# Differential and latent attention encoder on one core: score pairs, statistics without a diagonal, rotary halves summed in the contraction

## The chip, the cores and the metric

The kernel runs on one core of a Trainium2 chip. The metric is the time on the device in microseconds (us) from one launch to its end. PE is the matrix engine (PEld its weight loads), DVE the vector engine, ACT the scalar engine, POOL is GpSimd, SP the queue that issues the transfers.

## The reference

Two layers over 512 positions of width 1024, all in float32. Cut to what matters here:

```python
u = _rmsnorm(h, g_mix[l]); z = u @ w_in[l]
# latent group, 8 heads: 64 plain + 32 rotary columns per head
q = concat([q[..., :64], _rope(q[..., 64:], cos, sin)])
k = concat([kv[..., :64], broadcast(k_rope)])          # one rotary key for all heads
o_mla = softmax(q @ k.T * 96**-0.5) @ v
# differential group, 4 heads, two maps of 64 columns each
s = dq @ dk.T * 64**-0.5 - slope * abs(qpos - kpos)    # for map 0 and map 1
w = softmax(s[0]) - lam * softmax(s[1])
o = _rmsnorm(w @ dv, g_sub[l], 1e-5) * (1 - lam_init)
h = h + concat([o_mla, o_diff]) @ w_out[l]
h = h + square(relu(_rmsnorm(h, g_mlp[l]) @ w_up[l])) @ w_down[l]
```

`_rope(x)` is `[x1*cos - x2*sin, x1*sin + x2*cos]`. `lam` is one number per layer. A final norm follows the second layer.

## The kernel before

Every float32 product is made of three products of halves: an operand is split into a high part and the rest (`_hi`, `_lo`), and `three` (line 1145) issues hi*hi, hi*lo and lo*hi. Channels lie on the partitions and the 512 positions on the columns, so most matmuls are 128x128 stationary by 512 columns. The weights come block by block through two staging buffers; ACT writes the high half (line 520), DVE the low one (line 767).

A layer has these parts in time: projections of the latent compressions and of the values; the attention, as 48 steps of one head and one tile of 128 queries (steps 0 to 15 are the differential heads, 16 to 47 the latent ones); the rest of the output projection; the MLP. The order on each engine is written out by hand. In attention step n of the differential part, the engines do:

- PE, in program order: the scores of map 0 of step n+2 (`scores_diff(l, n + 2, 0)`), in some steps the broadcast of a statistic (`stat_b`), the filler work of the step (`FILL[n]`: projections of later heads, 12 matmuls in steps 0 to 7, 6 or none in later ones), in some steps the values of a head (`values`), the four transposes of step n-1 (`turn`, line 1206), the scores of map 1 of step n+2, in some steps the column sums of a statistic (`stat_c`, line 1159). In the latent part the scores of step n+2 (`scores`) stand first. Each map's scores are three matmuls with 64 rows: map 0 in partitions 0 to 63, map 1 in 64 to 127.
- DVE: `coef` (reciprocals of the two row sums, and lambda applied to the second, lines 810 and 811), two `ttr` (bias, negation and row extreme, line 803; each frees a score bank through `sc_free`), `weights` (line 817, after POOL), the low half of a transposed map (`lo_pt`, line 837), and the reading out of filler results (`gen`, `gen_low`).
- ACT: the high half of a transposed map (`hi_pt`, line 550), two exponentials (line 531), and its part of the fillers.
- POOL: `t1` (line 481) scales the second map by its coefficient; `power` (line 475) makes the inverse root of a statistic.

Three score banks and two transpose banks are shared by all steps. Two more banks take the fillers in turn, so that a filler waits (`taken`) until the result before it in its bank is read out.

A statistic is made in this chain: `stat_c` on PE, `stat_col` on DVE, `power` on POOL, `stat_diag` on DVE (line 788: four multiplications of the identity by a column, into `diag`), `stat_b` on PE (line 1168: ones times `diag`, 128x512), and the row is read out. It occurs 8 times in a layer; four of them are the norms of the differential heads, whose `stat_c` is at the end of steps 7, 11, 15 and 19 and whose `stat_b` is in steps 9, 13, 17 and 21.

For each latent head the query is read out by three DVE operations (`gen` with use "q"): a product of 96 rows with a table, a product of the 32 swapped rotary rows with the table (line 863), and the sum of the two (line 866).

`link` makes an instruction of DVE wait for the end of the one before it.

Of the kernel before, what the change touches and what calls it, by code (L numbers as in the profile page):

```python
# [12 lines left out]
P = 128  # L13
# [163 lines left out]
CHAIN = 3 + DSTEPS  # L177

def trunk(nc, x, w_in, g_mix, g_q, g_kv, w_uq, w_ukv, lam_q1, lam_k1, lam_q2, lam_k2,
# [53 lines left out]
    diag = place("diag", [P, TT, P], F32)  # L233
# [18 lines left out]
    with ExitStack() as ctx:  # L252
# [26 lines left out]
        pow_done, diag_ready = counter("pow_done", 4 + DIFF_HEADS), counter("diag_ready", 4 + DIFF_HEADS)  # L279

        c_ready, c_hi_made, c_lo_made = (counter(n, 2 * KC) for n in ("c_ready", "c_hi_made", "c_lo_made"))
        kr_half, kr_ready = counter("kr_half", 1), counter("kr_ready", 1)
# [5 lines left out]
        qf_ready, q_hi_made, q_lo_made = (counter(n, MLA_HEADS) for n in ("qf_ready", "q_hi_made", "q_lo_made"))  # L288
# [72 lines left out]
        def q_tile(hd):  # L361

            return q_pack[0:QK, (hd + 1) % 2, 0, :], q_pack[0:QK, (hd + 1) % 2, 1, :]
# [96 lines left out]
        def _(pool):  # L460
# [30 lines left out]
            for l in layers(pool):  # L491
                power(l, MISC_AT["mix_c"], 0, rs_mix)
                power(l, MISC_AT["q_c"], 1, rs)
                power(l, MISC_AT["kv_c"], 2, rs)
                for n in range(1, STEPS + 1):
                    if n <= DSTEPS:
                        t1(l, n - 1)
                    else:
                        normalise(l, n - 1 - DSTEPS)
                    g, r = divmod(n - 8, TT)  # L500
                    if r == 0 and 0 <= g < DIFF_HEADS:
                        power(l, MISC_AT[f"sub{g}_c"], 3 + g, rs)
                power(l, MISC_AT["mlp_c"], 3 + DIFF_HEADS, rs)
# [4 lines left out]
        def _(act):  # L508
# [44 lines left out]
            def gen(l, use):  # L553
# [75 lines left out]
            for l in layers(act):  # L629
# [32 lines left out]
                for n in range(STEPS + 5):  # L662
# [14 lines left out]
                    if n in (DSTEPS - 4, DSTEPS + 3):  # L677
                        for p in (0, 1) if n == DSTEPS - 4 else (2, 3):

                            act.wait_ge(kr_ready, val(kr_ready, l, 1))  # L680
# [3 lines left out]
                            nc.scalar.activation(k_pack[NOPE:QK, p, 0, :], krf[NOPE:QK, :], ACT.Copy  # L684
                                                 ).then_inc(krb_hi_made, 1)
                            if p:
                                act.wait_ge(krb_lo_made, val(krb_lo_made, l, 1))
                                nc.scalar.activation(k_pack[NOPE:QK, p, 1, :], k_pack[NOPE:QK, 0, 1, :].bitcast(F32),
                                                     ACT.Copy).then_inc(krb_copied, 1)
# [58 lines left out]
        def _(dve):  # L748
# [91 lines left out]
            def gen(l, use):  # L840
# [17 lines left out]
                elif use[0] == "q":  # L858
# [3 lines left out]
                    nc.vector.tensor_tensor(tmp_y[0:QK, 0, :], b[0:QK, :], tabq[0:QK, :], ALU.mult)  # L862
                    nc.vector.tensor_tensor(tmp_y[NOPE:QK, 1, :], b[QK:P, :], tabq[QK:P, :], ALU.mult
                                            ).then_inc(freed(use), 1)
                    dve.wait_ge(*read_out(l, use))
                    nc.vector.tensor_tensor(tmp_y[NOPE:QK, 0, :], tmp_y[NOPE:QK, 0, :], tmp_y[NOPE:QK, 1, :], ALU.add
                                            ).then_inc(qf_ready, 1)

            def gen_low(l, use):
# [21 lines left out]
                elif use[0] == "q":  # L891
                    hd = int(use[1:])
                    dve.wait_ge(q_hi_made, val(q_hi_made, l, hd + 1))
                    nc.vector.tensor_tensor(q_tile(hd)[1], tmp_y[0:QK, 0, :], q_tile(hd)[0].bitcast(F32), ALU.subtract
# [47 lines left out]
            for l in layers(dve):  # L942
# [6 lines left out]
                stat_diag(l, 0, rs_mix)  # L949
                stat_row(l, MISC_AT["mix_b"], rb[:, :])  # L950
                for k, use in enumerate(LATENT_USES):
# [7 lines left out]
                    else:  # L959
                        if l == 0:  # L960
# [13 lines left out]
                                                ).then_inc(kr_ready, 1)  # L974
                    split(l, k + RING)
                for b in range(TT):
                    split(l, BLOCK_AT[("dv", b)] + RING)
                    if b == 0:
# [4 lines left out]
                        stat_diag(l, 1, rs)  # L983
# [6 lines left out]
                    if b == 2:  # L990
# [5 lines left out]
                        stat_diag(l, 2, rs)  # L996
# [27 lines left out]
                for n in range(STEPS + 5):  # L1024
# [32 lines left out]
                    if n == DSTEPS - 4:  # L1057
                        dve.wait_ge(krb_hi_made, val(krb_hi_made, l, 1))
                        nc.vector.tensor_tensor(k_pack[NOPE:QK, 0, 1, :], krf[NOPE:QK, :],
                                                k_pack[NOPE:QK, 0, 0, :].bitcast(F32), ALU.subtract  # L1060
# [7 lines left out]
                    if r == 0 and 0 <= g < DIFF_HEADS:  # L1068
                        stat_diag(l, 3 + g, rs)
# [24 lines left out]
                stat_diag(l, 3 + DIFF_HEADS, rs)  # L1094
# [45 lines left out]
        def _(pe):  # L1140
# [23 lines left out]
            def stat_b(l, m, k):  # L1164

                pe.wait_ge(diag_ready, val(diag_ready, l, k + 1))
                pe.wait_ge(misc_free, val(misc_free, l, m))
                nc.tensor.matmul(MISC_BANK[:, :], ones[:, :], diag.rearrange("p t c -> p (t c)"), start=True, stop=True  # L1168
                                 ).then_inc(misc_done, 1)

            def scores_diff(l, n, m):

                hd, qt = divmod(n, TT)
                if qt == 0:
                    pe.wait_ge(d_lo_made, val(d_lo_made, l, 2 * hd + 2))
                e = 2 * n + m
                pe.wait_ge(sc_free, val(sc_free, l, e - 2))
                rows = slice(m * DIFF_D, (m + 1) * DIFF_D)
                three(SC_BANKS[e % 3][:, :],
                      [((dq_hi[rows, hd, qt * P:(qt + 1) * P], dq_lo[rows, hd, qt * P:(qt + 1) * P]),  # L1180
                        tuple(k[rows, :] for k in d_keys(hd)))], True, True).then_inc(sc_done, 1)

            def scores(l, n):
# [3 lines left out]
                if qt == 0:  # L1187
# [7 lines left out]
                        (k_pack[0:QK, hd % 4, 0, :], k_pack[0:QK, hd % 4, 1, :]))], True, True).then_inc(sc_done, 1)  # L1195
# [101 lines left out]
            for l in layers(pe):  # L1297
# [61 lines left out]
                scores_diff(l, 0, 0)  # L1359
                scores_diff(l, 0, 1)  # L1360
                scores_diff(l, 1, 0)
                scores_diff(l, 1, 1)
                head_sum(l, SECOND_USES[1], range(KD))
                for n in range(STEPS + 1):
                    if n + 2 < DSTEPS:
                        scores_diff(l, n + 2, 0)
                    elif n + 2 < STEPS:
                        scores(l, n + 2)
# [18 lines left out]
                    if n + 2 < DSTEPS:  # L1387
                        scores_diff(l, n + 2, 1)
# [125 lines left out]
```

## Time and profile before

| | |
|---|---|
| median of 3 runs | 1298.93 us (1298.62 to 1299.15) |
| profiled execution, its time | 1299.73 us |
| its span, first to last instruction | 1297.9 us |
| PE busy | 1253.6 us, 97% |
| DVE busy | 834.2 us, 64% |
| ACT busy | 515.7 us, 40% |
| POOL busy | 89.3 us, 7% |
| mean granted PE clock | 0.987 |

The profiled execution is 0.8 us above the median of the runs; 1.8 us of its time lie outside the span. PE's busy time is not a measure of how well it is used, since the time of one matmul overlaps that of the next. So its stretches are read by the distance from one start to the next.

### The profile page before, as it was taken

The page shows a single profiled execution, that of the slowest core. Times are in us where ns is not written, and L with a number is a line of the kernel's source. Part 1 is how long each engine was busy: PE and PEld are TensorE (multiplying, and loading weights), DVE is VectorE, ACT ScalarE, POOL GpSimd, SP SyncE. Part 2 cuts the span into 40 slices and gives each one's busy share as a digit, 9 for nine tenths or more (in the row PEclk, how much of TensorE's full clock was granted, in tenths as well). Part 3 has the DMA queues.
Part 4 walks back from the last instruction along what each step waited for, and adds up shares of the span by engine and source line. Part 5 has one row for each costly group of instructions (what it writes and reads, how often), then busy time and mean ns, then how long its engine had stood idle before and what let it go on. Part 6 is the DMA issues. An engine that isn't in the chain of part 4 may idle for free.

```text
span 1297.9 us, 15337 instructions
## 1 busy us (share of the span) xinstructions
PE 1253.6 (97%) x5675; PEld 1006.1 (78%) x5675; DVE 834.2 (64%) x1385; ACT 515.7 (40%) x848; POOL 89.3 (7%) x125
## 2 busy tenths in 40 slices
PE   5999989999999999999999999899999999999997
PEld 4877667778888888888888766587878888888886
DVE  5568878976845554555656688798675555555554
ACT  5245656654422222222333456666532222222223
POOL 0001212210000000000000012222000000000000
PEclk8999898999999999999999989999999999999999
DMA  5431100122433333333314210002233333333321
GB/s 167 113 81 57 33 1 17 34 81 65 131 97 97 97 97 98 98 98 97 97 54 114 58 53 13 17 17 66 84 88 105 98 97 97 97 98 97 97 82 65
DMA packets 142300, 102.39 MB, mean 79 GB/s; under 512 B 5346, under 2 KB 138516, under 8 KB 142228
## 3 DMA queue, kind: packets, MB, share of 16 engines
q1 hardware_dynamic: 142000, 101.40, 26.4%
q8 instruction: 46, 0.75, 0.2%
q14 instruction: 26, 0.21, 0.1%
q10 hardware_dynamic: 100, 0.03, 0.0%
q0 software_dynamic: 128, 0.00, 0.0%
HBM read 99.32 MB, written 2.10 MB: 78 GB/s over the span
## 4 chain that ended last, share of the span: by engine, by line
PE 59%; issue 28%; DVE 8%; ACT 2%; DMA 1%; POOL 1%; SPq 0%; POOLq 0%; DVEq 0%; ACTq 0%
PE bank L1145 54%; PE bank L1206 2%; PE bank L1227 2%; DVE pt_lo L837 2%; DVE nmx L824 1%; PE bank L1159 1%; ACT pt_hi L550 1%; DMA stage<-in_w_in 1%; DVE w_lo L767 1%; PE bank L1168 1%; PE bank L1321 1%; DVE k_pack L888 1%; DVE e_t L817 0%; DVE diag L788 0%; POOL rs L475 0%
## 5 line engine op out<-in xcount | busy, mean ns | idle before, releaser
L520 ACT ACTIVATE w_hi<-stage 128x1024 fp32r<-128x1024 f32 (+2 forms) x198 | 196.9, 1000 | 493.3 <-PE bank L1145 450.8
L1145 PE MATMUL bank<-u_hi,w_hi 128*128 128x512 f32 x768 | 305.9, 398 | 7.3 <-DVE u_lo L935 5.6
L1145 PE MATMUL bank<-u_hi,w_lo 128*128 128x512 f32 x768 | 300.0, 391 | 0.0
L1145 PE MATMUL bank<-u_lo,w_hi 128*128 128x512 f32 x768 | 299.9, 390 | 0.0
L767 DVE TENSOR_TENSOR w_lo<-stage,w_hi 128x1024 fp32r<-128x1024 f32 (+2 forms) x192 | 225.0, 1177 | 56.7 <-ACT w_hi L520 56.4
L1145 PE MATMUL bank<-hid_hi,w_hi 128*128 128x512 f32 x512 | 199.2, 389 | 0.0
L1145 PE MATMUL bank<-hid_lo,w_hi 128*128 128x512 f32 x512 | 199.2, 389 | 0.0
L1145 PE MATMUL bank<-hid_hi,w_lo 128*128 128x512 f32 x512 | 199.2, 389 | 0.0
L1145 PEld LDWEIGHTS bank<-u_hi,w_hi 128*128 128x128 f32 x768 | 144.7, 188 | 46.2 <-issue 17.5
L1115 DVE TENSOR_TENSOR h<-h,bank 128x512 f32<-128x512 f32 x128 | 87.7, 687 | 136.1 <-PE bank L1145 136.1
L1145 PEld LDWEIGHTS bank<-u_hi,w_lo 128*128 128x128 f32 x768 | 144.7, 188 | 30.9
L1145 PEld LDWEIGHTS bank<-u_lo,w_hi 128*128 128x128 f32 x768 | 144.8, 189 | 30.5 <-issue 1.4
L1104 DVE TENSOR_TENSOR tmp_y<-bank,rb 128x512 f32<-128x512 f32 x64 | 44.2, 690 | 123.8 <-PE bank L1145 123.7
L1145 PEld LDWEIGHTS bank<-hid_hi,w_lo 128*128 128x128 f32 x512 | 96.1, 188 | 20.1
L1145 PEld LDWEIGHTS bank<-hid_lo,w_hi 128*128 128x128 f32 x512 | 96.1, 188 | 20.0
L1145 PEld LDWEIGHTS bank<-hid_hi,w_hi 128*128 128x128 f32 x512 | 96.1, 188 | 19.8
L837 DVE TENSOR_TENSOR pt_lo<-bank,pt_hi 128x512 fp32r<-128x512 f32 x96 | 65.8, 685 | 37.7 <-ACT pt_hi L550 36.7
L550 ACT ACTIVATE pt_hi<-bank 128x512 fp32r<-128x512 f32 x96 | 56.8, 592 | 29.6 <-PE bank L1145 17.6
L1145 PE MATMUL bank<-k_pack,q_pack 96*128 96x512 f32 x192 | 61.4, 428 | 0.0
L734 ACT ACTIVATE hid_hi<-tmp_y 128x512 fp32r<-128x512 f32 x64 | 40.6, 634 | 45.4 <-DVE tmp_y L1107 45.3
L1206 PE MATMUL bank<-ident,e_t 128*128 128x128 f32 x344 | 52.2, 274 | 5.7 <-DVE pt_lo L837 5.7
L1206 PEld LDWEIGHTS bank<-ident,e_t 128*128 128x128 f32 x344 | 42.1, 141 | 19.5 <-issue 9.8
(174 smaller groups left out, 1522.9 us busy)
## 6 DMA issues: line engine op xcount, KB each, us to landing
stage<-in_w_up SPq DMA_DIRECT2D x64, 512.0 KB, 4.0
stage<-in_w_down SPq DMA_DIRECT2D x64, 512.0 KB, 3.4
stage<-in_w_in SPq DMA_DIRECT2D x32, 512.0 KB, 3.9
stage<-in_w_out SPq DMA_DIRECT2D x16, 512.0 KB, 3.4
xin<-in_x SPq DMA_DIRECT2D x4, 512.0 KB, 5.7
stage<-in_w_ukv SPq DMA_DIRECT2D x4, 512.0 KB, 3.2
out<-yout SPq DMA_DIRECT2D x4, 512.0 KB, 3.6
stage<-in_w_uq SPq DMA_DIRECT2D x4, 384.0 KB, 3.0
```

The source lines that it names most:

```text
L520: last = nc.scalar.activation(hi(w_hi, s)[:, :, d:d + n], st(r)[:, :, f:f + n], ACT.Copy)
L550: nc.scalar.activation(pt_hi[:, :, q * P:(q + 1) * P], TR_BANKS[n % 2].rearrange("p (k c) -> p k c", k=TT), ACT.Copy).then_inc(pt_hi_made, 1)
L734: nc.scalar.activation(hid_hi[:, c % 2, i, :], tmp_y[:, 1, :], ACT.Copy).then_inc(hid_hi_made, 1)
L767: last = nc.vector.tensor_tensor(dst, st(r)[:, :, f:f + n], hi(w_hi, s)[:, :, d:d + n].bitcast(F32), ALU.subtract)
L824: nc.vector.tensor_reduce(nmx[:, p_slot(i):p_slot(i) + 1], SC_BANKS[e % 3][:, :], AX_X, ALU.max, negate=True).then_inc(mx_ready, 1)
L837: nc.vector.tensor_tensor(piece(pt_lo), TR_BANKS[n % 2].rearrange("p (k c) -> p k c", k=TT), piece(pt_hi).bitcast(F32), ALU.subtract).then ...
L888: last = nc.vector.tensor_tensor(k_pack[0:NOPE, s, 1, :], b[p * NOPE:(p + 1) * NOPE, :], k_pack[0:NOPE, s, 0, :].bitcast(F32), ALU.subtract)
L1104: nc.vector.tensor_tensor(tmp_y[:, 0, :], bank[BANK[use]][:, :], rb[:, :], ALU.mult).then_inc(freed(use), 1)
L1115: nc.vector.tensor_tensor(h[:, j, :], h[:, j, :], bank[BANK[use]][:, :], ALU.add).then_inc(freed(use), 1)
L1145: mm = nc.tensor.matmul(acc, a, b, start=first and t == 0 and m == 0, stop=last and t == len(terms) - 1 and m == 2)
L1206: mm = nc.tensor.transpose(TR_BANKS[n % 2][:, kt * P:(kt + 1) * P], e_slot(t)[:, kt * P:(kt + 1) * P], ident[:, :])
L1227: mm = nc.tensor.matmul(MISC_BANK[:, :], v_pack[:, kt, hd, :, :].rearrange("p a c -> p (a c)"), pt[:, kt, :], start=(kt == 0 and pt is pt_ ...
```

## The change

1. `score_pair` takes the place of `scores_diff`: the six score matmuls of a step stand together, the maps taking turns, and they are issued for step n+1 after the fillers of step n, where before map 0 of step n+2 stood at the beginning of step n and map 1 at its end. Ahead of the loop, one pair is issued instead of two.
2. `stat_diag` and `diag` are gone. `stat_b` issues four matmuls whose stationary operand is a column of the statistic repeated 128 times, and whose moving operand is the identity, 128 columns each.
3. `coef` is one reciprocal; lambda is the second scalar of POOL's `t1`. POOL waits once for lambda ahead of the steps.
4. The query readout is one product of 128 rows. The rotary key stands twice in `k_pack` (rows 64 to 95 and 96 to 127), so the contraction over 128 rows forms the sum that DVE made. `krf` gets one more DVE operation per layer for it, and the copies and splits of the rotary key have 64 rows instead of 32.

```diff
@@ POOL @@
-                nc.gpsimd.tensor_scalar(e_slot(t), e_slot(t), coefs[:, t:t + 1], 1.0, ALU.mult, ALU.mult
+                nc.gpsimd.tensor_scalar(e_slot(t), e_slot(t), coefs[:, t:t + 1], cols(lam_b, 0, l), ALU.mult, ALU.mult
                                         ).then_inc(t1_ready, 1)
...
+                pool.wait_ge(lam_done, 2)
@@ ACT @@
-                    act.wait_ge(qf_ready, val(qf_ready, l, hd + 1))
+                    act.wait_ge(*read_out(l, use))
                     act.wait_ge(sc_done, val(sc_done, l, 2 * DSTEPS + TT * (hd - 1) if hd else 2 * (DSTEPS - TT)))
-                    nc.scalar.activation(q_tile(hd)[0], tmp_y[0:QK, 0, :], ACT.Copy).then_inc(q_hi_made, 1)
+                    nc.scalar.activation(q_tile(hd)[0], tmp_y[:, 0, :], ACT.Copy).then_inc(q_hi_made, 1)
@@ DVE @@
-            def stat_diag(l, k, src):
-                dve.wait_ge(pow_done, val(pow_done, l, k + 1))
-                for tt in range(TT):
-                    last = nc.vector.tensor_scalar(diag[:, tt, :], ident[:, :], src[:, tt:tt + 1], None, ALU.mult)
-                last.then_inc(diag_ready, 1)
...
-                link(l, nc.vector.reciprocal(coefs[:, t:t + 2], rsum[:, t:t + 2]))
-                nc.vector.tensor_scalar(coefs[:, t + 1:t + 2], coefs[:, t + 1:t + 2], cols(lam_b, 0, l), None, ALU.mult
-                                        ).then_inc(coef_ready, 1)
+                nc.vector.reciprocal(coefs[:, t:t + 2], rsum[:, t:t + 2]).then_inc(coef_ready, 1)
...
-                    nc.vector.tensor_tensor(tmp_y[0:QK, 0, :], b[0:QK, :], tabq[0:QK, :], ALU.mult)
-                    nc.vector.tensor_tensor(tmp_y[NOPE:QK, 1, :], b[QK:P, :], tabq[QK:P, :], ALU.mult
-                                            ).then_inc(freed(use), 1)
-                    dve.wait_ge(*read_out(l, use))
-                    nc.vector.tensor_tensor(tmp_y[NOPE:QK, 0, :], tmp_y[NOPE:QK, 0, :], tmp_y[NOPE:QK, 1, :], ALU.add
-                                            ).then_inc(qf_ready, 1)
+                    nc.vector.tensor_tensor(tmp_y[:, 0, :], b[:, :], tabq, ALU.mult).then_inc(freed(use), 1)
...
+                        nc.vector.tensor_tensor(krf[QK:P, :], krf[0:ROPE, :], ck[0:ROPE, :], ALU.add
+                                                ).then_inc(kr_ready, 1)
@@ PE @@
-                pe.wait_ge(diag_ready, val(diag_ready, l, k + 1))
+                pe.wait_ge(pow_done, val(pow_done, l, k + 1))
                 pe.wait_ge(misc_free, val(misc_free, l, m))
-                nc.tensor.matmul(MISC_BANK[:, :], ones[:, :], diag.rearrange("p t c -> p (t c)"), start=True, stop=True
-                                 ).then_inc(misc_done, 1)
-
-            def scores_diff(l, n, m):
+                src = rs if k else rs_mix
+                for tt in range(TT):
+                    mm = nc.tensor.matmul(MISC_BANK[:, tt * P:(tt + 1) * P], src[:, tt:tt + 1].to_broadcast([P, P]), ident[:, :],
+                                          start=True, stop=True)
+                mm.then_inc(misc_done, 1)
+
+            def score_pair(l, n):
...
-                e = 2 * n + m
-                pe.wait_ge(sc_free, val(sc_free, l, e - 2))
-                rows = slice(m * DIFF_D, (m + 1) * DIFF_D)
-                three(SC_BANKS[e % 3][:, :],
-                      [((dq_hi[rows, hd, qt * P:(qt + 1) * P], dq_lo[rows, hd, qt * P:(qt + 1) * P]),
-                        tuple(k[rows, :] for k in d_keys(hd)))], True, True).then_inc(sc_done, 1)
+                pe.wait_ge(sc_free, val(sc_free, l, 2 * n - 1))
+                q = slice(qt * P, (qt + 1) * P)
+                k_hi, k_lo = d_keys(hd)
+                for p, (a, b) in enumerate(((dq_hi, k_hi), (dq_hi, k_lo), (dq_lo, k_hi))):
+                    for m in range(2):
+                        rows = slice(m * DIFF_D, (m + 1) * DIFF_D)
+                        mm = nc.tensor.matmul(SC_BANKS[(2 * n + m) % 3][:, :], a[rows, hd, q], b[rows, :],
+                                              start=p == 0, stop=p == 2)
+                        if p == 2:
+                            mm.then_inc(sc_done, 1)
...
-                scores_diff(l, 0, 0)
-                scores_diff(l, 0, 1)
-                scores_diff(l, 1, 0)
-                scores_diff(l, 1, 1)
+                score_pair(l, 0)
                 head_sum(l, SECOND_USES[1], range(KD))
                 for n in range(STEPS + 1):
-                    if n + 2 < DSTEPS:
-                        scores_diff(l, n + 2, 0)
-                    elif n + 2 < STEPS:
+                    if DSTEPS < n + 2 < STEPS:
                         scores(l, n + 2)
...
+                    if n + 1 < DSTEPS:
+                        score_pair(l, n + 1)
                     if r == 0 and g >= 0:
                         values(l, g)
                     if n:
                         turn(l, n - 1)
-                    if n + 2 < DSTEPS:
-                        scores_diff(l, n + 2, 1)
+                    if n + 2 == DSTEPS:
+                        scores(l, n + 2)
                     if r == 1 and 0 <= g < DIFF_HEADS:
                         stat_c(l, MISC_AT[f"sub{g}_c"], tmp_s[:, 1, :])
```

## Rows read from the trace of the kernel before

**Rows 1.** The page: busy time by engine, and PE's clock in 40 slices

```profile
PE 1253.6 (97%) x5675; PEld 1006.1 (78%) x5675; DVE 834.2 (64%) x1385; ACT 515.7 (40%) x848; POOL 89.3 (7%) x125
...
PEclk8999898999999999999999989999999999999999
```

**Rows 2.** Windows: stretch, length, busy us (instructions) of PE, PEld, DVE, ACT, POOL, clock, DMA

```profile
91.00:137.50 46.50, 46.31 (x225) 33.83 (x223) 34.39 (x87) 25.31 (x58) 5.58 (x8) 1.00 0.19 57
108.00:125.00 17.00, 17.00 (x89) 12.56 (x88) 16.63 (x43) 11.76 (x31) 2.79 (x4) 1.00 0.23 77
137.50:207.00 69.50, 60.01 (x263) 42.74 (x263) 57.72 (x135) 41.57 (x89) 14.31 (x18) 0.90 0.04 12
140.30:147.00 6.70, 5.26 (x11) 3.18 (x12) 6.63 (x19) 3.30 (x8) 1.38 (x2) 0.50 0.05 16
207.00:287.00 80.00, 79.20 (x396) 63.57 (x395) 69.19 (x127) 51.66 (x105) 18.13 (x26) 1.00 0.17 53
768.40:837.50 69.10, 59.83 (x267) 42.17 (x267) 57.49 (x135) 41.49 (x90) 14.31 (x18) 0.93 0.05 15
```

**Rows 3.** Chain that ended last, steps 2 and 3 of layer 0

```profile
112.47 3.86 PE bank L1145 x18
116.77 3.86 PE bank L1145 x18
```

**Rows 4.** Timeline of PE: a step's score matmuls, and the first scores of layer 0

```profile
91.56 0.50 PE L1145 MATMUL bank<-dk_hi,dq_hi 64*128 64x512 f32 x2
...
94.30 0.50 PE L1145 MATMUL bank<-u_hi,w_hi 128*128 128x512 f32 x1
...
112.41 0.51 PE L1145 MATMUL bank<-dk_hi,dq_hi 64*128 64x512 f32 x2
...
112.97 0.40 PE L1145 MATMUL bank<-dk_hi,dq_lo 64*128 64x512 f32 x2
113.31 0.50 PE L1145 MATMUL bank<-u_hi,w_hi 128*128 128x512 f32 x1
```

**Rows 5.** Chain of waits, 137 to 207 us

```profile
138.83 1.03 POOL rs L475
...
139.89 0.87 DVE diag L788 x4
...
140.87 0.04 DVE coefs L811
...
149.37 0.71 DVE tmp_y L863
...
150.10 0.68 DVE tmp_y L866
...
156.02 0.97 PE bank L1145 x3
...
164.09 0.70 DVE k_pack L888
...
164.84 1.66 PE bank L1145 x6
```

**Rows 6.** Groups of DVE, 137.5 to 207 us: busy us, mean ns, idle before

```profile
L788 DVE TENSOR_SCALAR diag<-ident,rs 128x128 f32<-128x128 f32 x16 | 3.5, 282 | 2.0 <-POOL rs L475 2.0
L863 DVE TENSOR_TENSOR tmp_y<-bank,consts 32x512 f32<-32x512 f32 x4 | 2.8, 696 | 0.1
...
L866 DVE TENSOR_TENSOR tmp_y<-tmp_y 32x512 f32<-32x512 f32 x4 | 2.7, 682 | 0.1
...
L811 DVE TENSOR_SCALAR coefs<-coefs,lam_b 128x1 f32<-128x1 f32 x8 | 1.7, 214 | 0.3
```

**Rows 7.** Groups of the whole run: busy us, mean ns, idle before

```profile
L1168 PE MATMUL bank<-diag,ones 128*128 128x512 f32 x32 | 21.0, 743 | 3.0 <-DVE diag L788 3.0
...
L481 POOL TENSOR_SCALAR e_t<-e_t,coefs 128x512 f32<-128x512 f32 x22 | 15.3, 697 | 141.0 <-DVE coefs L811 141.0
...
L1159 PE MATMUL bank<-ones,ss 128*128 128x1 f32 x72 | 8.5, 239 | 0.0
```

More of the change, by code:

```diff
@@ L174, in previous @@
     return max(a for a in range(NBLK) if slots[a] == slots[b]) - NBLK
-CHAIN = 3 + DSTEPS
+CHAIN = 3
 def trunk(nc, x, w_in, g_mix, g_q, g_kv, w_uq, w_ukv, lam_q1, lam_k1, lam_q2, lam_k2,
@@ L278, in trunk @@
         sq_ready, ss_acc = counter("sq_ready", 2 * KD + 2 * KC), counter("ss_acc", 2 * KD + 2 * KC)
-        pow_done, diag_ready = counter("pow_done", 4 + DIFF_HEADS), counter("diag_ready", 4 + DIFF_HEADS)
+        pow_done = counter("pow_done", 4 + DIFF_HEADS)
         c_ready, c_hi_made, c_lo_made = (counter(n, 2 * KC) for n in ("c_ready", "c_hi_made", "c_lo_made"))
-        kr_half, kr_ready = counter("kr_half", 1), counter("kr_ready", 1)
+        kr_half, kr_ready = counter("kr_half", 1), counter("kr_ready", 2)
         krb_hi_made, krb_lo_made, krb_copied = counter("krb_hi_made", 4), counter("krb_lo_made", 1), counter("krb_copied", 3)
@@ L287, in trunk @@
         v_hi_made, k_hi_made = counter("v_hi_made", TT), counter("k_hi_made", MLA_HEADS)
-        qf_ready, q_hi_made, q_lo_made = (counter(n, MLA_HEADS) for n in ("qf_ready", "q_hi_made", "q_lo_made"))
+        q_hi_made, q_lo_made = (counter(n, MLA_HEADS) for n in ("q_hi_made", "q_lo_made"))
         sc_done, sc_free = (counter(n, 2 * DSTEPS + MSTEPS) for n in ("sc_done", "sc_free"))
@@ L361, in q_tile @@
         def q_tile(hd):
-            return q_pack[0:QK, (hd + 1) % 2, 0, :], q_pack[0:QK, (hd + 1) % 2, 1, :]
+            return q_pack[:, (hd + 1) % 2, 0, :], q_pack[:, (hd + 1) % 2, 1, :]
         def p_slot(i):
@@ L678, in _ @@
                         for p in (0, 1) if n == DSTEPS - 4 else (2, 3):
-                            act.wait_ge(kr_ready, val(kr_ready, l, 1))
+                            act.wait_ge(kr_ready, val(kr_ready, l, 2))
                             act.wait_ge(sc_done, val(sc_done, l, 2 * (DSTEPS - TT)))
@@ L683, in _ @@
                                 act.wait_ge(misc_done, val(misc_done, l, MISC_AT[f"pv{DIFF_HEADS - 1}"] + 1))
-                            nc.scalar.activation(k_pack[NOPE:QK, p, 0, :], krf[NOPE:QK, :], ACT.Copy
+                            nc.scalar.activation(k_pack[NOPE:P, p, 0, :], krf[NOPE:P, :], ACT.Copy
                                                  ).then_inc(krb_hi_made, 1)
@@ L687, in _ @@
                                 act.wait_ge(krb_lo_made, val(krb_lo_made, l, 1))
-                                nc.scalar.activation(k_pack[NOPE:QK, p, 1, :], k_pack[NOPE:QK, 0, 1, :].bitcast(F32),
+                                nc.scalar.activation(k_pack[NOPE:P, p, 1, :], k_pack[NOPE:P, 0, 1, :].bitcast(F32),
                                                      ACT.Copy).then_inc(krb_copied, 1)
@@ L893, in gen_low @@
                     dve.wait_ge(q_hi_made, val(q_hi_made, l, hd + 1))
-                    nc.vector.tensor_tensor(q_tile(hd)[1], tmp_y[0:QK, 0, :], q_tile(hd)[0].bitcast(F32), ALU.subtract
+                    nc.vector.tensor_tensor(q_tile(hd)[1], tmp_y[:, 0, :], q_tile(hd)[0].bitcast(F32), ALU.subtract
                                             ).then_inc(q_lo_made, 1)
@@ L1058, in _ @@
                         dve.wait_ge(krb_hi_made, val(krb_hi_made, l, 1))
-                        nc.vector.tensor_tensor(k_pack[NOPE:QK, 0, 1, :], krf[NOPE:QK, :],
-                                                k_pack[NOPE:QK, 0, 0, :].bitcast(F32), ALU.subtract
+                        nc.vector.tensor_tensor(k_pack[NOPE:P, 0, 1, :], krf[NOPE:P, :],
+                                                k_pack[NOPE:P, 0, 0, :].bitcast(F32), ALU.subtract
                                                 ).then_inc(krb_lo_made, 1)
@@ L1067, in _ @@
                             gen(l, use)
-                    if r == 0 and 0 <= g < DIFF_HEADS:
-                        stat_diag(l, 3 + g, rs)
                     if r == 1 and g >= DIFF_HEADS and (g - DIFF_HEADS) % 2 == 1 and g < DIFF_HEADS + MLA_HEADS - 1:
@@ L1194, in scores @@
                       [(tuple(q[:, qt * P:(qt + 1) * P] for q in q_tile(hd)),
-                        (k_pack[0:QK, hd % 4, 0, :], k_pack[0:QK, hd % 4, 1, :]))], True, True).then_inc(sc_done, 1)
+                        (k_pack[:, hd % 4, 0, :], k_pack[:, hd % 4, 1, :]))], True, True).then_inc(sc_done, 1)
             def turn(l, n):
```

5 lines of the change are left out of this document (removed).

## The prediction

> **What bounds the kernel now.** I read the page first, then windows, then the chain of waits and the timeline where the windows differ. The page gives PE 97% busy at the full clock nearly everywhere [rows 1]. That says PE is the engine to look at, but not that each stretch is bound by it, since one matmul's time overlaps the next. The windows split the attention of a layer in three [rows 2].
>
> - Steps 0 to 7, 91 to 137.5 us: PE idles 0.2 us of 46.5. A step of 12 filler matmuls, 6 score matmuls and 4 transposes starts every 116.77 - 112.47 = 4.30 us [rows 3]. PE bounds it, though DVE shows 16.63 us in 17 [rows 2].
> - Steps 7 to 21, 137.5 to 207 us: PE is idle 9.5 us of 69.5 and the clock is 0.90; from 140.3 to 147.0 it is 0.50, the lower of its two levels, while DVE shows 6.63 us of 6.70 [rows 2]. The chain of waits runs here through POOL's power, DVE's diagonal, the query readout and the key readout, one behind the other [rows 5]. This is bound by DVE and by hand-overs. Layer 1 has the same stretch, 69.1 us long at clock 0.93 [rows 2].
> - Steps 21 to 46, 207 to 287 us: PE idles 0.8 us of 80 at full clock [rows 2]. PE bounds it, and so it does in the rest of the layer.
>
> So removed DVE work is worth time in some 70 us of each layer, and removed PE time everywhere.
>
> **The change, part by part.** All sums are per layer.
>
> *Score pairs, the interleaving itself.* At the end of step n map 1 of step n+2 (rows 64 to 127) already stands right before map 0 of step n+3 (rows 0 to 63). The timeline shows their six matmuls as three double starts, at 112.41 and later, and the next filler at 113.31: six in 0.90 us [rows 4]. A filler matmul takes (4.30 - 0.90 - 0.53) / 12 = 0.24 us, with 0.53 an estimate for the transposes; six in series would take over 1.4 us. The halves run side by side already, so taking turns gains nothing: 0.
>
> The Trainium skill (TensorE: Matmul & The Clock Gate, Part 3, "The mechanism") has matmuls of different row groups run together, but says they keep program order. By that rule the three of map 1 would go first and the three of map 0 behind them with only one pair overlapping, and the new order would save some 0.45 us in about 11 steps, 5 us a layer. The rows show the halves starting together without it, and the measurement decides.
>
> *Fewer blocks of scores.* Ahead of the loop, 12 score matmuls take 94.30 - 91.56 = 2.74 us, with a wait for DVE in them [rows 4]. One pair takes 0.90. Since the pair of step n+1 comes in step n, a pair is in every step then: through the first transposes PE issues 2.74 + 0.90 (map 0 of step 2 alone) + 0.90 before, and 3 x 0.90 after: -1.84 us. It is in the PE-bound stretch, so it shows in full. Behind it, a statistic's column sums stand between the two maps and split a pair; the split half costs 0.97 us at 156.02 on the chain [rows 5] and is gone: -0.9 us. Step 7 has such a split too, but PE waits for DVE right behind it, so I count it at 0.
>
> *Statistics.* PE: the 128x512 product takes two passes (x32 for 16) and some 0.43 us each, 0.86 us [rows 7]. The new form is four products of 128 columns, eight passes; column sums, also eight passes but of one column, have a mean of 239 ns overlapped [rows 7]. Same columns; the loads add nothing if they hide, and at most 0.3 us a piece if they don't. 0, upper end +2.4 us for eight. DVE: 4 x 0.282 us overlapped, 0.87 us per statistic [rows 5, 6]. Three of the four in steps 7 to 21 are on the chain: -2.6 us. The diagonal also waited for POOL, 2.0 us in all [rows 6], once on the chain behind POOL's 1.03 us [rows 5]: -1.0 us. What is late next is PE's own wait for the power before `stat_b`; in steps 9, 13, 17 and 21 the fillers and transposes are queued behind it, so 0 to +1.3 us comes back. The other four diagonals lie beside full PE work: 0.
>
> *Lambda.* DVE's small operation and the link cost 140.87 to 141.00, 0.13 us, up to 0.21 [rows 5, 6]. 8 are in the stretch, some 6 on the chain: -0.8 us. POOL's `t1` has a second scalar from memory instead of an immediate. No row has that form. Below: 697 ns, no change [rows 7]. Above: DVE's operations with a scalar from memory take some 0.75 us where those without take 0.69, an estimate of +0.1 us. I take 0, since POOL is idle most of the time.
>
> *Query readout.* Two operations fall away, 0.71 + 0.68 from start to start 1.41 us [rows 5]. Four heads are read out in steps 7 to 21 (x4 in [rows 6]); two lie on the chain: -2.8 us. The other four lie in the PE-bound stretch; they help the waits left there, 0.8 us [rows 2]: -0.4 us. Contraction over 128 rows instead of 96 has the same 512 columns: 0. The rotary key's extra operation, 0.68 us, is beside the value projection on PE: 0; uncovered it would cost 0.7.
>
> *Shorter lookahead.* Scores are issued one step ahead instead of two. In a full step, DVE can start the first `ttr` of step n when the pair ends, before the transposes; the next pair comes 0.53 + 12 x 0.24 = 3.4 us later and needs that `ttr`, which takes 0.7 and a hand-over of 0.2: 2.5 us of slack. DVE's steps alternate around 3.4 and 4.6 us of starts against 4.30 (some 4.0 on average, an estimate from 16.63 us in 17 with each operation overlapping a tenth), so it lags at most some 1.3 us: 0 in steps 0 to 7. In the steps without fillers (8, 10, 14) nothing covers the wait and PE idles where DVE was ahead before.
>
> *Sum for steps 7 to 21:* 0.9 + 2.6 + 1.0 + 0.8 + 2.8 = 8.1 us. Not all can come: a second limit stands close behind. At 164.09 the key's low half holds a filler's bank, and the filler starts at 164.84 [rows 5]; with a faster DVE the filler before is earlier and waits longer for the same ACT and DVE pieces. Following the new order through steps 7 to 21 with these durations, I find PE waiting 1.0 to 2.6 us at five places, about as many us as before. I keep 0.8 of the sum: 6.5 us. The clock is counted as before, about two low stretches a layer.
>
> Per layer 1.8 + 6.5 + 0.4 = 8.7 us, for two layers 17.4. The profiled execution is 1299.7 us (span 1297.9 and 1.8 around it), 0.8 above the median; 1299.7 - 17.4 = 1282.3, against the median 1281.5. I say 1282.
>
> **Rivals.**
>
> - *The clock stays high.* Two low stretches a layer cost some 3 us each in steps 7 to 21 (6.7 us at half speed [rows 2]). If denser work keeps the clock up and the whole sum comes, the layer gains 1.8 + 8.1 + 0.4 + 2.5 = 12.8: 1273. For: the stretch has the same work in less time. Against: column sums, short blocks and waits remain, and those preceded the fall.
> - *Hand-overs, not DVE's work.* ACT's high halves and bank releases take over at once, and only PE's own part (1.8) and 1 to 2 us of the rest come: 3.5 a layer, 1292. For: the chain changes engine often [rows 5]. Against: from 138.8 to 155 us it hardly leaves DVE.
> - *The shorter lookahead decides*, the other sign. If DVE comes to the first `ttr` of a step more than 2.5 us late, the pair waits, the transposes wait behind it, and DVE's next `ttr` behind those. The gain is gone at 17.4 / 28 = 0.6 us of wait in each of 28 steps, so from a lateness of 3.1 us. With 1.2 us of wait a step it is 34 us: 1316. For: DVE is nearly full there [rows 2]. Against: the slack above.
> - *The seams were not shared*: if the maps ran in series at the seams of before and the new order makes them run together, about 11 steps gain 0.45 us more each: 10 us for both layers, 1272. Against: the double starts at 112.41 [rows 4]. This is what the named page's program order would make of it.
> - *Nothing to see*: the DVE work is off the path and the waits eat PE's part: 1298.9 within 0.2%.
>
> **How the numbers follow.** Chances: forecast (1277 to 1289) 0.61; clock 0.13; hand-overs 0.13; seams 0.02; nothing 0.04; lookahead 0.07. 0.2% or 2.6 us is about what a measurement can tell from no change. The first four are faster, 0.89; same 0.04; slower 0.07. The range takes the forecast and most of the two beside it: 1273 to 1292 leaves out the two last and the ends of the others. The unknown costs (8 x 0.3 us of loads a layer, +1.3 of waits a statistic) lie within it.
>
> **What would show it.** Right: the first transposes of each layer 1.8 us earlier; full steps still 4.30 us apart; six score matmuls in 0.90 us; no line 788, 811, 863 and 866; `stat_b` some 0.9 us; steps 7 to 21 some 63 us long instead of 69.5; the stretch behind it unchanged to within 0.5 us. Wrong: PE waits on line 803 in steps 1 to 6 (lookahead); `t1` well over 0.7 us; a low clock in other places, or nowhere; six matmuls in less than 0.90 us (the interleaving would gain after all, up to 5 us a layer).

## The result, and the profile after

The changed kernel takes 1283.31 us (median of 4 runs, 1281.66 to 1283.96) against 1298.94 before: a ratio of 0.9874, 95% interval 0.9862 to 0.9885, or 15.6 us less. Forecast were 1282 and a range from 1273 to 1292. A second measurement beside other kernels gave 0.9878 (0.9863 to 0.9893).

The profiled execution is the fastest of the four, 1281.66 us. Busy times and PE's clock from its page, to be read against [rows 1]:

```profile
PE 1235.6 (97%) x5771; PEld 1006.2 (79%) x5771; DVE 792.5 (62%) x1259; ACT 515.5 (40%) x848; POOL 90.2 (7%) x125
...
PEclk9999999999999999999999999999999999999999
```

DVE's busy time fell by 41.7 us, the time by less than half of that. PE is 97% busy as before, which again says nothing of where the time went. The windows of the same three parts of the attention do (columns as in [rows 2]):

```profile
90.30:132.80 42.50, 42.50 (x213) 31.15 (x212) 30.87 (x73) 23.98 (x54) 6.05 (x8) 1.00 0.18 55
132.80:199.50 66.70, 56.15 (x300) 42.98 (x299) 50.07 (x110) 42.87 (x92) 14.85 (x20) 0.95 0.05 16
158.70:162.10 3.40, 3.40 (x12) 1.82 (x10) 0.63 (x2) 0.00 (x0) 0.77 (x1) 0.50 0.00 0
199.50:272.00 72.50, 72.25 (x366) 58.78 (x365) 59.83 (x114) 50.12 (x102) 17.61 (x26) 1.00 0.17 52
756.50:821.60 65.10, 54.52 (x299) 42.26 (x298) 50.04 (x110) 42.86 (x92) 14.79 (x20) 0.97 0.06 17
```

The middle part of layer 0 is 66.7 us long. It is cut at the first transposes of steps 7 and 22 on PE, which are those of maps 6 and 21. By the same marks it was 207.34 - 136.07 = 71.3 us before. The two windows of before, for this part and for the one behind it:

```profile
136.07:207.34 71.27, 61.78 (x272) 43.79 (x271) 59.49 (x139) 43.22 (x92) 14.45 (x19) 0.90 0.05 16
207.30:281.20 73.90, 73.10 (x367) 58.51 (x366) 66.47 (x123) 49.98 (x102) 18.13 (x26) 1.00 0.16 51
```

DVE does 59.5 - 50.1 = 9.4 us less in the middle part. PE is idle 10.5 us of it, where it was 9.5. The clock is 0.95 instead of 0.90: a low stretch of 3.4 us at 158.7 and one of 3.4 us at 192.8, in place of two of 6.8 us.

The waits of PE in this part, each with its releaser, the number of times and the longest:

```profile
PE bank L1128 <- DVE k_pack L875: 2.9, 1, 2.9
PE bank L1196 <- DVE pt_lo L829: 2.8, 2, 2.3
PE bank L1128 <- DVE tmp_s L1036: 2.1, 2, 1.1
PE bank L1168 <- DVE nmx L797: 1.5, 2, 1.3
PE bank L1128 <- DVE v_pack L868: 0.5, 1, 0.5
PE bank L1153 <- POOL rs L474: 0.4, 1, 0.4
```

The wait for a diagonal is gone and POOL's power holds PE for 0.4 us only. The largest wait is a filler behind the key's low half (0.5 us at most before). And one has come in that PE did not have before: the values of a head behind line 1036, DVE's product with a statistic.

The groups that the change touches, to be read against [rows 7]:

```profile
L480 POOL TENSOR_SCALAR e_t<-e_t,coefs,lam_b 128x512 f32<-128x512 f32 x22 | 16.9, 767 | 130.7 <-DVE coefs L804 130.7
...
L1153 PE MATMUL bank<-ident,rs 128*128 128x128 f32 x112 | 16.6, 296 | 0.9 <-POOL rs L474 0.9
...
L1128 PE MATMUL bank<-k_pack,q_pack 128*128 128x512 f32 x192 | 60.4, 424 | 0.0
```

The last line is the scores of the latent heads, contracted over 128 rows. Over 96 rows, before, they took as long:

```profile
L1145 PE MATMUL bank<-k_pack,q_pack 96*128 96x512 f32 x192 | 61.4, 428 | 0.0
```

And the score pairs on PE's timeline, in a full step [rows 4]:

```profile
112.17 0.50 PE L1168 MATMUL bank<-dk_hi,dq_hi 64*128 64x512 f32 x2
112.50 0.40 PE L1168 MATMUL bank<-dk_lo,dq_hi 64*128 64x512 f32 x2
112.74 0.40 PE L1168 MATMUL bank<-dk_hi,dq_lo 64*128 64x512 f32 x2
113.06 0.66 PE L1196 MATMUL bank<-ident,e_x 128*128 128x128 f32 x4
113.47 0.47 PE L1128 MATMUL bank<-u_hi,w_hi 128*128 128x512 f32 x1
```

Six score matmuls in 113.06 - 112.17 = 0.89 us, as at the seams of before.

Where the 18.1 us between the two profiled executions came from is read from the first transpose of a step in both timelines. Map 0, 6, 21 and 47 are turned at the marks; us:

| stretch | before | after | gain |
|---|---|---|---|
| layer 0, start to map 0 | 107.59 | 104.59 | 3.00 |
| maps 0 to 6 | 28.49 | 28.21 | 0.28 |
| maps 6 to 21 | 71.26 | 66.68 | 4.58 |
| maps 21 to 47 | 73.82 | 72.51 | 1.31 |
| to map 0 of layer 1 | 458.18 | 456.25 | 1.93 |
| maps 0 to 6 | 28.49 | 28.21 | 0.28 |
| maps 6 to 21 | 69.70 | 65.17 | 4.53 |
| maps 21 to 47 | 74.72 | 72.50 | 2.22 |

The rest of the run, behind map 47 of layer 1, is as long as before to within 0.1 us.

Of the first 3.00 us, about 1.0 is not the change's: 0.16 is an earlier start, and 0.87 is the clock. The chain of waits has these two lines at the start, before and after, for the first 48 matmuls:

```profile
19.46 13.37 PE bank L1145 x48
```

```profile
19.30 12.50 PE bank L1128 x48
```

The clock was at its lower level for 6.8 us there before and for 3.4 us after. Another profiled execution of the changed kernel had 6.8 us too, and the median is 1.65 us above the execution profiled here.

### The profile page after: what moved, and what is told of

Same layout as the page of the kernel before. It is cut to its first block, busy times and chain, and to the rows that moved or that the text cites. A ratio compares the mean times of both kernels' runs of the same rounds, so it can differ in the third digit from the quotient of the medians.

```text
span 1279.9 us, 15395 instructions
## 1 busy us (share of the span) xinstructions
PE 1235.6 (97%) x5771; PEld 1006.2 (79%) x5771; DVE 792.5 (62%) x1259; ACT 515.5 (40%) x848; POOL 90.2 (7%) x125
## 4 chain that ended last, share of the span: by engine, by line
PE 63%; issue 28%; DVE 4%; ACT 3%; DMA 1%; SPq 0%; POOL 0%; POOLq 0%; DVEq 0%; ACTq 0%
PE bank L1128 55%; PE bank L1196 3%; PE bank L1217 2%; PE bank L1168 1%; DVE pt_lo L829 1%; ACT pt_hi L550 1%; DMA stage<-in_w_in 1%; PE bank L1153 1%; PE bank L1311 1%; PE bank L1142 0%; ACT w_hi L520 0%; DVE e_t L809 0%; DVE tmp_s L1036 0%; DVE w_lo L767 0%; ACT e_x L531 0%
## 5 line engine op out<-in xcount | busy, mean ns | idle before, releaser
L1128 PE MATMUL bank<-k_pack,q_pack 128*128 128x512 f32 x192 | 60.4, 424 | 0.0
```

Of the source, the lines that this page charges most:

```text
L1128: mm = nc.tensor.matmul(acc, a, b, start=first and t == 0 and m == 0, stop=last and t == len(terms) - 1 and m == 2)
```

## The experiments

Each was timed beside the kernel before, which came out at 1299.92, 1300.06 and 1299.36 us in the three groups of runs. So versions of different groups are compared by their ratio to it. Of the parts alone, each edit is that part of the diff, put on the kernel before.

**The score pairs alone** (`scores_diff` replaced by `score_pair`, with the new loop):

```diff
-                scores_diff(l, 0, 0)
-                scores_diff(l, 0, 1)
-                scores_diff(l, 1, 0)
-                scores_diff(l, 1, 1)
+                score_pair(l, 0)
...
+                    if n + 1 < DSTEPS:
+                        score_pair(l, n + 1)
```

> The kernel before with the score pairs alone. If the parts add up as in the prediction, 1.8 us ahead of the first transposes and up to 0.9 us in steps 7 to 21 come back per layer: 5 us, about 1294. If the shorter lookahead hurts in steps 7 to 21 as long as DVE is still slow, some of it is lost: 1296 to 1299.

1299.88 us, ratio 0.9999 (0.9990 to 1.0007): nothing. The gain ahead of the loop is there (458.18 us from layer 0's map 47 to layer 1's map 0 became 455.98, and 28.49 became 28.23 and 28.21). Maps 6 to 21 took 71.50 and 73.93 us instead of 71.26 and 69.70. PE's waits in that part of layer 1:

```profile
PE bank L1168 <- DVE diag L788: 3.0, 4, 1.4
PE bank L1145 <- DVE k_pack L888: 3.0, 1, 3.0
PE bank L1210 <- DVE pt_lo L837: 2.8, 2, 2.3
PE bank L1182 <- DVE nmx L803: 2.1, 1, 2.1
PE bank L1145 <- DVE tmp_s L1050: 1.6, 2, 1.1
```

This is the second of the expected cases, at its upper end (the kernel before took 1299.92 us beside it): what the pairs gain ahead of the steps is given back in them. The clock does not explain it. The low stretches in the middle parts of both layers add to 23.9 us here and to 23.9 us before, and the two parts together are 4.5 us longer. This is the rival of the shorter lookahead, in steps 7 to 21 instead of 0 to 7.

**Everything but the score pairs:**

> Everything but the score pairs (statistics, lambda, query readout), with the old order of the scores. By the prediction steps 7 to 21 give 5.6 us a layer and the rest 0.4: about 1287. If the old lookahead of two steps was worth something to a faster DVE, these steps shrink by more than in the changed kernel (over 4.6 us a layer) and the time is 1285 or less; if DVE's work was not what bound the stretch, 1291 to 1295.

1285.72 us, ratio 0.9891 (0.9878 to 0.9905), against 0.9874 for the whole change. The pairs add some 2 us to it, but the intervals overlap. The time lies between the two expected cases, 1287 and 1285 or less. Maps 6 to 21 took 66.12 and 65.51 us, together the same as in the changed kernel (66.68 and 65.17), but for another reason:

```profile
136.10:202.20 66.10, 62.53 (x296) 48.34 (x295) 49.27 (x108) 42.54 (x92) 15.04 (x19) 0.87 0.05 17
761.40:827.00 65.60, 61.16 (x296) 47.06 (x295) 49.16 (x108) 42.64 (x92) 15.05 (x20) 0.90 0.05 17
```

PE idles 3.6 and 4.4 us instead of 10.5, and the clock is 0.87 and 0.90 instead of 0.95 and 0.97. The execution spent 17 us of the middle part of layer 0 at the lower level. PE's waits there (136 to 202 us) are:

```profile
PE bank L1192 <- DVE pt_lo L829: 2.3, 1, 2.3
PE bank L1128 <- DVE v_pack L868: 0.7, 1, 0.7
PE bank L1142 <- ACT tmp_s L591: 0.6, 2, 0.3
```

With the old order of the scores, the waits for the key's low half (2.9 us in the changed kernel) and for line 1036 (2.1 us) are not there (in layer 1 a wait of 0.9 us for the key is). With the new order and the old DVE work (the pairs alone, above) they are. So these waits come with the order of the scores. Against the changed kernel, waits were traded for a slow clock; which of the two would be left if the other went was not tried.

**The maps in series in each pair:**

```diff
-                for p, (a, b) in enumerate(((dq_hi, k_hi), (dq_hi, k_lo), (dq_lo, k_hi))):
-                    for m in range(2):
+                for m in range(2):
+                    for p, (a, b) in enumerate(((dq_hi, k_hi), (dq_hi, k_lo), (dq_lo, k_hi))):
```

> The changed kernel with the three matmuls of map 0 ahead of the three of map 1 in each pair. If the halves run side by side whatever their order, as the trace of before showed at its seams: six matmuls in 0.90 us and the changed kernel's 1283. If program order holds them apart, each pair takes about 1.3 us and 32 pairs cost 10 to 14 us: 1294 to 1297.

1284.11 us, ratio 0.9885 (0.9870 to 0.9900), the changed kernel's time. The timeline of the step shown above:

```profile
112.65 0.50 PE L1168 MATMUL bank<-dk_hi,dq_hi 64*128 64x512 f32 x2
112.98 0.40 PE L1168 MATMUL bank<-dk_lo,dq_hi 64*128 64x512 f32 x2
113.22 0.40 PE L1168 MATMUL bank<-dk_hi,dq_lo 64*128 64x512 f32 x2
113.54 0.66 PE L1196 MATMUL bank<-ident,e_x 128*128 128x128 f32 x4
```

Double starts again and 0.89 us for six, although all of map 0 stands ahead of all of map 1. Taking turns is worth nothing that can be measured.

**The query readout alone:**

> The kernel before with the query readout alone (one product of 128 rows, the rotary key twice). Predicted 2.8 us in steps 7 to 21 and 0.4 behind them per layer: about 1292.5. If the waits behind it are set by ACT and by banks, half of that: 1296.

1293.80 us, ratio 0.9958 (0.9945 to 0.9970): 5.5 us. The low stretches of the clock add to the same 23.9 us in the middle parts as before. Maps 6 to 21 gave only 1.9 and 0.7 us of the 2.8 predicted for each layer; maps 21 to 47 gave 1.3 and 2.2 us of a predicted 0.4, and they took 72.5 us in both layers as in the changed kernel:

```profile
205.40:278.00 72.60, 72.35 (x367) 58.85 (x366) 60.17 (x114) 50.16 (x102) 17.93 (x26) 1.00 0.17 52
833.80:906.30 72.50, 72.25 (x366) 58.80 (x365) 60.14 (x114) 50.10 (x102) 17.92 (x26) 1.00 0.16 52
```

**The statistics alone:**

> The kernel before with the statistics alone: columns repeated, no diagonal. Predicted 2.6 + 1.0 us a layer on the path of steps 7 to 21: about 1293 by the sum, four fifths of it 1294. If the path goes round the diagonals through ACT and the banks, half of that or less: 1296 to 1299. If the loads of a repeated column don't hide, stat_b takes over 1.2 us instead of 0.9.

1295.06 us, ratio 0.9956 (0.9943 to 0.9970): 5.7 us with an interval of 3.9 to 7.4. That total is the four fifths that were expected. Maps 6 to 21 gave 2.1 and 1.9 us in the profiled execution, little more than half of the 3.6 us a layer of the sum, with 27.3 us of low clock in them where the kernel before had 23.9.

**Lambda alone:**

> The kernel before with lambda moved to GpSimd alone. Predicted 0.8 us a layer, 1.6 us in all, and t1 at 0.70 us as before; if a second scalar from memory costs 0.05 us or more, it shows in t1's mean. From the other parts measured (5.5 us for the readout, 5.7 for the statistics, 14.1 for the three together) some 3 us are left for it: 1297.

1295.92 us, ratio 0.9974 (0.9965 to 0.9983): 3.4 us, 2.2 to 4.5, where 1.6 was predicted. Maps 6 to 21 gave 2.5 and 0.6 us. `t1` has a mean of 768 ns here and 767 in the changed kernel, against 697 before [rows 7]: the second scalar from memory costs GpSimd 0.07 us, and the kernel gains nevertheless.

**A product moved ahead on DVE** (the changed kernel; line 1036 to the beginning of steps 10, 14 and 18):

```diff
                     if read_pt and pt_first:
                         lo_pt(l, n - 3)
+                    g, r = divmod(n - 8, TT)
+                    if n in (10, 14, 18):
+                        dve.wait_ge(misc_done, val(misc_done, l, MISC_AT[f"sub{g}_b"] + 1))
+                        nc.vector.scalar_tensor_tensor(out=tmp_s[:, 0, :], in0=tmp_s[:, 0, :], scalar=cols(gsl, 0, l),
...
                     if 0 < n <= DSTEPS:
                         coef(l, n - 1)
...
-                    if r == 2 and 0 <= g < DIFF_HEADS:
+                    if n == 22:
```

> The changed kernel with DVE's multiplication by the statistic (line 1036) moved from behind weights to the beginning of steps 10, 14 and 18. Theory: in the changed kernel the next head's values wait for it while it is queued behind coef, ttr and weights. If so, the transposes of steps 9 and 13 come 1 to 2 us earlier and the layer ends 2 to 4 us earlier: 1276 to 1280. Rival: DVE's order only moves the wait to ttr, and the time is 1282 to 1285.

1283.77 us, ratio 0.9864 (0.9845 to 0.9883), with runs from 1278.4 to 1286.7: the time that the rival names, but too scattered to tell. Step 13 became 0.9 and 1.1 us shorter as the theory says (map 13 after map 12: 5.73 and 5.71 to 4.84 and 4.63), but the profiled execution had low stretches in step 9 of layer 0 and step 12 of layer 1, which became 1.0 and 1.5 us longer.

**The pair of step 14 ahead of the filler of step 13:**

```diff
+                    if n == 13:
+                        score_pair(l, n + 1)
                     for use, part in FILL.get(n, []):
...
-                    if n + 1 < DSTEPS:
+                    if n + 1 < DSTEPS and n != 13:
                         score_pair(l, n + 1)
```

> The changed kernel with the pair of step 14 ahead of the filler in step 13. Theory: there the filler waits for the bank that the key's low half holds and the pair is queued behind it, so DVE starves. If so, steps 12 and 13 together (14.15 us in layer 0, 12.6 in layer 1) shrink by 1.5 to 2.5 us a layer: 1279 to 1281. Rival: the key's readout on ACT and DVE sets these steps by itself, no change: 1283.

1279.30 us, ratio 0.9840 (0.9826 to 0.9853), against 0.9874 and 0.9878 for the changed kernel: 4 us faster. Maps 6 to 21 took 64.16 and 64.26 us. Steps 12 and 13 together went from 14.15 and 12.61 to 11.72 and 11.77 us, 2.4 and 0.8 us less where 1.5 to 2.5 was expected. In a second execution of the changed kernel they took 14.00 and 13.49. The theory holds: one pair queued behind one filler that waits for a bank costs some 2 us a layer. The place in the changed kernel (columns as in [rows 4], idle time and releaser in brackets):

```profile
154.82 0.39 PE L1153 MATMUL bank<-ident,rs 128*128 128x128 f32 x2
158.10 0.50 PE L1128 MATMUL bank<-w_hi,c_hi 128*128 128x512 f32 x1 [2.90 <-DVE k_pack L875]
...
160.49 1.22 PE L1168 MATMUL bank<-dk_last,dq_hi 64*128 64x512 f32 x4
161.51 0.63 PE L1168 MATMUL bank<-dk_last,dq_lo 64*128 64x512 f32 x2
162.07 0.66 PE L1196 MATMUL bank<-ident,e_t 128*128 128x128 f32 x4
```

The pair waits from 155 to 160.5 us. The banks that it needs were free when DVE had read map 0 of step 13, at 154.4 us, and DVE runs out of scores behind it:

```profile
153.76 0.69 DVE L797 CUSTOM_DVE_ANT_0 e_t<-bank,consts 128x512 f32<-128x512 f32 x1
...
162.17 0.69 DVE L797 CUSTOM_DVE_ANT_0 e_x<-bank,consts 128x512 f32<-128x512 f32 x1 [2.85 <-PE bank L1168]
```

The clock falls for 3.4 us at 158.7, behind the idle time of 2.9 us.

**Pairs two steps ahead** (the changed kernel; the pair of step n+2 behind the transposes of step n):

```diff
                 score_pair(l, 0)
                 head_sum(l, SECOND_USES[1], range(KD))
+                score_pair(l, 1)
...
-                    if n + 1 < DSTEPS:
-                        score_pair(l, n + 1)
...
                         stat_c(l, MISC_AT[f"sub{g}_c"], tmp_s[:, 1, :])
+                    if n + 2 < DSTEPS:
+                        score_pair(l, n + 2)
```

> The changed kernel with its pairs issued two steps ahead, behind the transposes of step n for step n+2. If the shorter lookahead costs the changed kernel something in steps 7 to 21 (12 of 14 steps leave DVE waiting for scores in some), this shrinks them below 66.7 and 65.2 us by 1 to 3 us: 1278 to 1281. If PE's fillers matter more than DVE's scores there, it is as before without the split pairs: 65 to 67 us and 1283 to 1285.

1278.76 us, ratio 0.9833 (0.9820 to 0.9847). Maps 6 to 21 took 63.66 and 64.73 us, 3.0 and 0.4 us less than in the changed kernel. PE is idle 9.2 us of this part in layer 0, where it was 10.5. The largest waits:

```profile
PE bank L1196 <- DVE pt_lo L829: 2.3, 1, 2.3
PE bank L1128 <- DVE tmp_s L1036: 2.0, 2, 1.1
PE bank L1128 <- DVE k_pack L875: 1.7, 1, 1.7
PE bank L1168 <- DVE nmx L797: 1.4, 2, 1.2
```

**The changed kernel and this version, side by side:**

> The changed kernel once more beside the others of this call: 1282 to 1284, ratio to before 0.987.

> The version with pairs two steps ahead once more: if its gain over the changed kernel is real, again 3 to 5 us below it (1278 to 1280); if it was the chip, equal to it.

1283.46 us (1282.86 to 1284.12) and 1278.68 us (1277.73 to 1279.80), ratios 0.9878 (0.9863 to 0.9893) and 0.9841 (0.9827 to 0.9854). The runs do not overlap: 4.8 us are real. Maps 6 to 21 took 67.32 and 65.77 us in the one, 63.71 and 63.73 us in the other. In layer 1 both had 6.8 us at the lower clock, so these 2.0 us are lookahead alone.

**Both moves together:**

> Pairs two steps ahead and DVE's multiplication by the statistic at the beginning of steps 10, 14 and 18. With scores ready early, moving the multiplication ahead should let the values of heads 1 and 2 start earlier: step 9, 8.0 us in the version without it, shrinks by 1 us or more and the time is 1276 to 1278. Rival: as in the changed kernel with the move alone (1283.8), it gives nothing: 1279.

1278.80 us, ratio 0.9841 (0.9826 to 0.9856): nothing beyond pairs two steps ahead. The move of line 1036 is worth nothing that can be measured. Step 9, expected to shrink from 8.0 us, took 6.2 and 7.7 us. The 8.0 us had a low stretch of the clock in them, and so had the 7.7. Where there was none, the step took 6.6 us without the move (second execution, both layers) and 6.2 with it.

**The clock beside the times.** The middle parts (maps 6 to 21) of both layers together, and the time that PE was at the lower level in them, one profiled execution each; us:

| version | middle parts | of it at the lower clock |
|---|---|---|
| before | 141.0 | 23.9 |
| pairs alone | 145.4 | 23.9 |
| readout alone | 138.3 | 23.9 |
| statistics alone | 137.0 | 27.3 |
| lambda alone | 137.8 | 27.3 |
| all but the pairs | 131.6 | 30.7 |
| changed kernel | 131.9 | 10.2 |
| changed kernel, second execution | 133.1 | 17.1 |
| pair of step 14 first | 128.4 | 13.7 |
| pairs two steps ahead | 128.4 | 13.7 |
| the same, second execution | 127.4 | 13.7 |

A stretch at half clock can cost up to half its length, as the first 48 matmuls of the run show (last section). So the clock is up to (23.9 - 10.2) / 2 = 6.8 us of the 9.1 us that the changed kernel gained here in the first execution, and up to 3.4 of 7.9 us in the second.

## Why the prediction was right, point by point

The sum of 17.4 us stands against 15.6 measured. By place, for a layer in the profiled execution, 1.8 us were forecast ahead of the steps and in steps 0 to 6, 6.5 in steps 7 to 21 and 0.4 behind them. Measured were 2.2 (with the 1.0 us of the start left out), 4.6 and 1.8. So two of the three places came out wrong, in opposite directions. Its terms, per layer:

- *What bounds the kernel.* Right for PE in steps 0 to 7. Too generous for steps 21 to 46: I read 0.8 us of idle PE from the window and took it for all there was to gain. From start to start they were 73.8 and 74.7 us long and are 72.5 now, so 1.3 and 2.2 us were lost there. A matmul of 512 columns is 0.39 us long in the trace and the next one starts 0.23 us after it. So a start can come 0.16 us late without any idle time to show for it, and PE's busy time fell too, by 0.85 us in layer 0 for the same matmuls (from 73.10 to 72.25 us in the windows shown). By these starts the term of 0.4 us should have been 1.8. The prediction's own sign of being right, "unchanged to within 0.5 us", failed here.
- *Interleaving, 0.* Right, and shown: in series the pairs take the same 0.89 us. The Trainium skill (TensorE: Matmul & The Clock Gate, Part 3, "The mechanism") says that matmuls of different row groups overlap, and that they start in program order. The first holds here; the second does not describe the starts in these traces, where the first matmuls of the two halves start 0.01 us apart although two more of map 0 stand between them.
- *Fewer blocks of scores, 1.8 us ahead of the loop.* Right: 1.93 us for layer 1 in the profile, and 458.18 - 455.98 = 2.2 with the pairs alone. Not foreseen: with the pair between fillers and transposes a full step takes 4.24 instead of 4.30 us, 0.28 us over six steps; 4.30 was named as a sign.
- *The 0.9 us for the split pair, and the shorter lookahead at 0.* This step failed. I priced the lookahead for full steps, where it costs nothing (no wait on line 797 in the first part, and full steps of 4.24 us). For steps 7 to 21 I wrote that PE idles where DVE was ahead, named the steps without fillers (8, 10, 14), and gave it no term. Pairs alone lost 0.2 and 4.2 us in them, 2.2 a layer at an unchanged sum of low clock; two steps of lookahead in the changed kernel give 4.8 / 2 = 2.4 us a layer back. So the two terms together are a cost of some 2.3 us in place of a gain of 0.9. What the split pair is worth by itself was not measured. Most of the cost is one place, step 13, as moving its pair shows. That step has a filler, and the pair is late because the filler in front of it waits for its bank, not because DVE is late for the pair.
- *Statistics.* The cost on PE was right: the eight passes have a mean near 0.3 us, and 0.89 us stand on the chain instead of 0.86. The upper end of 0.3 us a statistic for the loads came from no row, and 0.03 us were measured. For DVE, 3.6 us were predicted on the path of steps 7 to 21 and the part alone gives 5.7 us for both layers, 2.9 a layer. That is four fifths of the sum, as forecast; of it, 2.0 us a layer lie in those steps in the profiled execution, which had more low clock there.
- *Lambda, 0.8 us a layer.* Too small: measured 1.1 to 2.2 by the part alone. Why it is more than the 0.13 to 0.21 us of the operation, six times, was not looked into. `t1` became 0.07 us longer, inside the bounds (0 to 0.1) and not the 0 that I took.
- *Query readout, 2.8 + 0.4 us.* 5.5 us for both layers, 2.8 a layer against 3.2: the size was right and the place wrong. 1.9 and 0.7 us came in steps 7 to 21, and 1.3 and 2.2 in the part behind it.
- *The next limit.* Right in kind: steps 7 to 21 gave 4.6 and 4.5 us (3.9 and 3.9 in the second execution) instead of 8.1 by the plain sum and 6.5 as forecast, and PE is idle in them as long as before (10.5 against 9.5 us).
- *The clock.* Counted as before; it was better. Low stretches in the middle parts add to 6.8 and 3.4 us in the profiled execution and to 10.2 and 6.8 us in the second, against 13.7 and 10.2 before. The rival that the clock stays high came true in part and covers part of what the lookahead cost. How the gain of the whole change divides between clock and waits is not settled, since it changes both. For the pairs alone and the readout alone it is: their low time is that of before.

So that the total came out near was luck in part: a term with the wrong sign (the lookahead and the split pair, off by 3.2 us a layer) was set off by three that were too small: the part behind step 21, lambda, and the clock. What the prediction had right is that DVE's work in steps 7 to 21 was on the path. The parts alone sum to 0.0 + 5.5 + 5.7 + 3.4 = 14.6 us, the three without the pairs give 14.2 together and the whole 15.6 to 16.4.

## What to carry to other kernels

In a queue written out by hand, whatever stands behind an instruction that waits for a buffer waits with it: before moving work to a later place, look in each step for what the work now in front of it can wait for. Check slack in the thin steps as well as in the full ones; here a shift that was free in seven full steps cost 2.3 us a layer in the thin ones, and putting one pair of matmuls ahead of one filler gave some 4 of the 5 us back. Idle time from a window understates what PE loses to waits, so compare the starts of the same instruction from step to step. And add up the time at the lower clock beside each time that is compared: two versions here took the same time in the same steps, one with waits and one with a slow clock.

## What the runs showed of the hardware

- Two row halves of the array run side by side even when three matmuls of one half stand ahead of three of the other in the program: 0.89 us for six in both orders.
- GpSimd's multiplication of 128x512 takes 0.70 us with one scalar from memory and an immediate, and 0.77 us with two from memory.
- A column repeated 128 times as stationary operand costs hardly more than other weights: eight passes of 128 columns in 0.89 us, against 0.86 us for two of 512.
- PE's clock went to its lower level, 1.2 GHz, for 3.4 or 6.8 us at a time in the middle parts. In the profiled execution of the changed kernel it fell three times there, 0.4 to 1.3 us behind the end of waits of PE of 2.9, 2.3 and 2.3 us (at 158.7, 192.8 and 814.0 us). In that of the kernel before it fell at 140.3 us, during a wait of 1.7 us.
- In the first 48 matmuls of the run the low clock costs half of the time that it covers: 12.50, 12.77 and 13.37 us for them with 2.8, 3.4 and 4.7 us of them at the lower level (the changed kernel twice, and the kernel before). Less half of that, each is 11.0 to 11.1 us. The same program had a low stretch of 3.4 us there in one execution and of 6.8 us in another.
